# A two-layer hybrid decoder on one core: the order of the trunk's phases rewritten, and short attention tiles joined

## The reference, cut to what matters

```python
for l in range(DEPTH):
    h = rms_norm(x, norm1_w[l])
    proj = h @ w_in[l]
    z, xbc, dt_raw, sb_qkv, nsa_q, nsa_kv, nsa_gate = jnp.split(proj, IN_SPLITS, axis=-1)
    y_ssd = ssd_mixer(z, xbc, dt_raw, ...)                     # conv, state space scan in chunks of 128, gated norm
    y_sb = rms_norm(stick_breaking_attention(sb_qkv), ...)     # 4 heads
    y_nsa = rms_norm(nsa_attention(nsa_q, nsa_kv, ...), ...)   # compressed + selected + window branch, 4 heads
    x = x + jnp.concatenate([y_ssd, y_sb, y_nsa], axis=-1) @ w_out[l]
    x = x + peer_ffn(rms_norm(x, norm2_w[l]), ...)
```

## Time and profile before

| what | value |
|---|---|
| median of 3 runs | 3233.42 us (3232.33 to 3233.64) |
| the profiled execution | 3229.1 us, its span 3227.3 us |
| busy share of the span | PE 79%, DVE 75%, POOL 66%, ACT 25% |
| moved by DMA | 1187.51 MB, mean 368 GB/s; gathers 1073.87 MB of it |
| TensorE's granted clock, mean | 0.911 of 2.4 GHz |

### The profile page before, as it was taken

The page is one execution under the profiler, slowest core; times in us unless marked ns, Lnnn a source line. Parts: engine busy times, 40 slices in busy tenths (PEclk is TensorE's granted clock), DMA queues, the critical chain, the costliest instruction groups (busy, mean ns, idle before and its releaser), DMA issues. The chain is left out here.

```text
span 3227.3 us, 30187 instructions
## 1 busy us (share of the span) xinstructions
PE 2555.5 (79%) x8860; PEld 1512.6 (47%) x8860; DVE 2429.2 (75%) x5632; ACT 799.3 (25%) x1853; POOL 2115.9 (66%) x2059
## 2 busy tenths in 40 slices
PE   8877677898897686888788687899898587656667
PEld 7666433665464332665455342566566342222222
DVE  2324997768878997768878998758877999666664
ACT  2521222234321122223421122233431122111111
POOL 0001677657777777757776777766777777777775
PEclk9859799999898899898899799999899899998889
DMA  5104899999999999999999999999999999999999
GB/s 191 55 21 160 345 409 409 412 406 372 383 379 411 366 402 410 411 411 394 397 392 410 390 404 409 410 412 388 386 376 411 393 385 409 409 409 410 409 409 354
DMA packets 311313, 1187.51 MB, mean 368 GB/s; under 512 B 34544, under 2 KB 34544, under 8 KB 298352
## 3 DMA queue, kind: packets, MB, share of 16 engines
q0 software_dynamic: 294912, 1073.87, 84.7%
q1 hardware_dynamic: 16240, 111.72, 8.7%
HBM read 1183.36 MB, written 2.10 MB: 367 GB/s over the span
## 5 line engine op out<-in xcount | busy, mean ns | idle before, releaser
L754 PE MATMUL acc<-v_rows,diag 128*128 128x512 f32 x2728 | 1431.5, 659 | 485.7 <-DMA v_rows<-expert_v,idx 391.1
L1416 DVE CUSTOM_DVE_ANT_0 u_rows<-u_rows,h 128x1024 f32<-128x1024 f32 x1024 | 1231.4, 1216 | 398.4 <-DMA u_rows<-expert_u,idx 396.4
L1477 POOL DMA_INDIRECT u_rows<-expert_u,idx x1024 | 1057.0, 1032 | 625.6 <-DVE idx L1381 269.0
L1490 POOL DMA_INDIRECT v_rows<-expert_v,idx x1024 | 1057.2, 1032 | 425.6 <-issue 261.1
L754 PEld LDWEIGHTS acc<-v_rows,diag 128*128 128x128 f32 x2728 | 523.3, 207 | 1202.2 <-issue 985.4
L1434 DVE SCALAR_TENSOR_TENSOR X<-v_rows,wgt,X 128x1024 f32<-128x1024 f32 x342 | 439.2, 1284 | 43.5 <-DMA v_rows<-expert_v,idx 37.9
L1032 ACT ACTIVATE diag<-consts,wgt 128x128 f32<-128x128 f32 x682 | 255.1, 395 | 746.9 <-PE acc L754 567.9
L465 PE MATMUL bank<-HT,w_ring 128*128 128x256 f32 x1792 | 412.6, 386 | 2.2 <-DVE HT L1040 2.2
L465 PEld LDWEIGHTS bank<-HT,w_ring 128*128 128x128 f32 x1792 | 350.0, 196 | 93.3 <-issue 46.1
L474 PE MATMUL bank<-w_ring,HT 128*128 128x256 f32 (+1 forms) x1280 | 278.7, 375 | 2.6 <-ACT arena L765 2.6
L765 ACT ACTIVATE arena<-bank 128x256 f32<-128x256 f32 (+4 forms) x304 | 112.7, 382 | 664.5 <-PE bank L465 253.8
(11 more groups left out here) (185 smaller groups left out, 1990.6 us busy)
## 6 DMA issues: line engine op xcount, KB each, us to landing
w_ring<-weights SPq DMA_DIRECT2D x100, 1024.0 KB, 8.0
u_rows<-expert_u,idx POOLq DMA_INDIRECT x1024, 11.0
v_rows<-expert_v,idx POOLq DMA_INDIRECT x1024, 11.2
X<-in_x SPq DMA_DIRECT2D x2, 1024.0 KB, 6.6
out<-X SPq DMA_DIRECT2D x4, 512.0 KB, 6.6
n2w_wide<-parameters SPq DMA_DIRECT2D x2, 512.0 KB, 8.4
params<-parameters SPq DMA_DIRECT2D x2, 412.0 KB, 7.6
consts<-constants SPq DMA_DIRECT2D x1, 749.5 KB, 6.4
```

The lines of the kernel that those rows point to most:

```text
L754: last = T.matmul(acc[:, at_h], diag[:, i % DIAG_RING], v_rows[:, t % V_RING, at_h], start=(at_t == 0), stop=(t == max(q for q in range(t ...
L1416: made(V.tensor_tensor_reduce(out=rows_u, in0=rows_u, in1=h2[:], scale=1.0, scalar=0.0, op0=ALU.mult, op1=ALU.add, accum_out=dots[:, b % 2 ...
L1477: pool.indirect_dma_start(out=u_rows[:, s % U_RING, :], out_offset=None, in_=u_dram, in_offset=bass.IndirectOffsetOnAxis(ap=idx[:, n % 2, ...
L1490: pool.indirect_dma_start(out=v_rows[:, t % V_RING, :], out_offset=None, in_=v_dram, in_offset=bass.IndirectOffsetOnAxis(ap=idx[:, t // PE ...
```

## The change

It keeps the computation and rewrites the order, with what the order needs:

- `UNITS`: the projections come as keys and queries (`na`), stick-breaking q and k, the values, then the state space's features and the gate z; the weight slots are renumbered, and the compressed tokens' weights become slot 7 instead of 12.
- The evacuation of unit j becomes a phase of its own, `e{j}`, which may stand elsewhere than at `u{j+1}`.
- `phases(n)` has one list for step 0 (FIRST_UNITS, then FIRST_ATT with the attention tiles between its strings) and one for steps 1 to 3 (BESIDE_UNITS by pair, then BEFORE_ATT, then attention). Stick-breaking, keys and compressed tokens stand between the projections in all steps. In step 0 the state space's hops stand between the attention tiles; in steps 1 to 3 they stand ahead of them.
- `att_tiles`: in pair 0 tiles are joined, 4 heads of a 128-wide block or 2 heads of a 256-wide one, so 16 tiles become 6 (11 phases in place of 21); in pair 1 they stay 16. A tile's scores are now the mask first (one matmul over all its heads), then per head one matmul for the earlier columns and one for the block's own.
- Stick-breaking in pair 0: `sl` handles two heads at once (two Abs, two Exp, two Ln: one pair of table switches for two heads), and `wT` has two buffers.
- `y5`: the two Ln run together, then the two Exp; the norm of the sparse attention (`rstd("4")`) runs once for both blocks.
- Scratch tiles move to other memory, the compressed keys' sum takes the fourth bank, and some waits change with them (`cz` no longer waits for the state space's end; `de00` and `y5` wait for the compressed tokens).

The core of the diff:

```diff
-UNITS = ([("f", m) for m in range(8)] + [("z", 0, 0), ...] + [("f", m) for m in range(8, 12)]
-         + [("sv", 0), ("sv", 1), ("kv", 0), ("kv", 1)] + [("na", 0, 0), ...])
+UNITS = ([("na", 0, 0), ("na", 1, 0), ("na", 0, 1), ("na", 1, 1)] + [("f", m) for m in range(8, 12)]
+         + [("sv", 0), ("sv", 1), ("kv", 0), ("kv", 1)] + [("f", m) for m in range(8)]
+         + [("z", 0, 0), ("z", 1, 0), ("z", 0, 1), ("z", 1, 1)])
+FIRST_UNITS = (
+    "u0 u1 u2 u3 u4 np0 u5 np1 u6 np2 u7 np3 u8 np4 u9 sz0 sz1 nt0 u10 sl0 sl1 ne0 nt1 u11 sp0 sp1 ne1 u12 sr0 cz dt0 u13 sr1 se0 "
+    "cm0 cm1 cm2 cm3 se1 u14 so0 cr dt1 sw0 u15 so1 ct sz2 sz3 sw1 cv0 dt2 u16 sl2 sl3 k0 cv1 dt3 u17 sp2 sp3 k1 dt4 cv2 u18 sr2 k2 "
+    "dt5 cv3 u19 sr3 se2 kt cv4 se3 u20 so2 ke cv5 sw2 u21 so3 cs cv6 cs0 cs1 sw3 u22 cx0 cv7 cs2 cs3 cs4 u23 cs5 cs6 cs7 ca")
+BESIDE_UNITS = [
...
+    "u0 u1 u2 u3 u4 np0 u5 np1 u6 np2 u7 np3 u8 np4 u9 nt0 ne0 e9 u10 nt1 ne1 e10 cz sz0 u11 sl0 e11 dt0 sp0 u12 sr0 dt1 e12 se0 so0 "
+    "sz1 sw0 u13 sl1 dt2 e13 sp1 dt3 u14 dt4 sr1 e14 se1 dt5 cm0 cm1 cm2 cm3 cr so1 ct k0 sw1 sz2 u15 sl2 k1 cv0 e15 sp2 u16 sr2 cv1 k2 e16 "
...
+    "cv7 u22 e22 u23 e23 cs0 cs1 cs2 cs3 cs4 cs5 cs6 cs7"]
+BEFORE_ATT = ("xt0 dl00 xe0 de00 xt1 dl01 xe1 de01 xp0 xp1 cb0 dm0 yp0 ya0 dl10 ys0 st0 de10 su0 dl11 cb1 de11 dm1 yp1 ya1 st1 ys1 su1 "
+              "y2 y3 y5")
+FIRST_ATT = ["xt0 dl00", "xe0 de00 cx1 xt1 dl01", "xe1 de01 xp0 cp cb0", "xp1 dm0 ce yp0", "ya0 ys0 oc dl10", "og de10 dl11 st0",
+              "de11 su0 cb1", "dm1", "yp1", "ya1 ys1 st1", "su1 y2 y3", "y5"]
...
+        tiles = {1: [[0, 2, 4, 6], [1, 3, 5, 7]], 2: [[0, 2], [1, 3], [4, 6], [5, 7]]}.get(2 * p + b + 1, [[i] for i in range(8)])
...
-                        T.matmul(out[:, 0:width], nqT[base:base + 64, h // 2, blk[b]], nkT[base:base + 64, br, 0:width], start=True, stop=False)
-                        full(T.matmul(out[:, here[b]], ident, const("causal_neg"), start=False, stop=True), f"{n}.s{k}")
+                        T.matmul(out[:, :, here[b]], ident, const("causal_neg").unsqueeze(1).to_broadcast([P, len(heads), P]),
+                                 start=True, stop=False)
+                        for at_h, i in enumerate(heads):
+                            for cut in ([slice(0, width - P)] if width > P else []) + [here[b]]:
+                                last = T.matmul(out[:, at_h, cut], nqT[base:base + 64, i % NSA_H // 2, blk[b]],
+                                                nkT[base:base + 64, i // NSA_H, cut], start=False, stop=(...))
...
             def stick_l():
-                for h in range(SB_H):
-                    yield f"sl{h}"
+                at_once = 2 - p
+                for first in range(0, SB_H, at_once):
+                    yield f"sl{first + at_once - 1}"
```

More of the change, by code:

```diff
@@ L157, in phases @@
-def phases():
-    head = [("n1a", 0, .3), ("n1b", 0, 0), ("n1c", 0, .3), ("n1t0", 1.8, 0), ("n1t1", 1.8, 0), ("n1e0", 0, 1.3), ("n1e1", 0, 1.3)]
[L160 to L176, removed]
@@ new lines, in of_heads @@
+def of_heads(b, heads):
+    step = heads[1] - heads[0] if len(heads) > 1 else 1
+    return slice(8 * b + heads[0], 8 * b + heads[-1] + 1, step)
+ATT = [att_tiles(p) for p in range(PAIRS)]
+LAST_OF = [[max(k for k, tile in enumerate(ATT[p]) if tile[0] == b) for b in range(2)] for p in range(PAIRS)]
+FIRST_UNITS = (
[3 rows of a table added]
+BESIDE_UNITS = [
[8 rows of a table added]
+BEFORE_ATT = ("xt0 dl00 xe0 de00 xt1 dl01 xe1 de01 xp0 xp1 cb0 dm0 yp0 ya0 dl10 ys0 st0 de10 su0 dl11 cb1 de11 dm1 yp1 ya1 st1 ys1 su1 "
+              "y2 y3 y5")
@@ L186, in phases @@
     tail += [("g2", 0, .5)]
[L187 to L195, removed]
-def slots():
[L201 to L205, removed]
+    return head + costed(units) + att + tail
+PHASES = [phases(n) for n in range(STEPS)]
+ORDER = [{name: i for i, (name, *_) in enumerate(of_step)} for of_step in PHASES]
+assert all(len(a) == len(b) for a, b in zip(ORDER, PHASES))
+BEGINS = [0, *(int(n) for n in np.cumsum([len(of_step) for of_step in PHASES]))]
+def slots():
+    out = []
+    for n in range(STEPS):
+        first = ORDER[n]["r8"]
+        work = np.array([max(cost) + .5 for _, *cost in PHASES[n][:first]] + [cost[1] + .5 for _, *cost in PHASES[n][first:]])
+        spread = lambda part, lo, hi: lo + (np.cumsum(part) - part) / part.sum() * (hi - lo)
+        if n:
+            of_step = spread(work[:first], TRUNK_AT - PER_STEP, FIRST_AT - PER_STEP), spread(work[first:], FIRST_AT - PER_STEP, ROUTED_AT)
+        else:
+            of_step = np.full(first, -1), spread(work[first:], 1, ROUTED_AT)
+        out.append(n * PER_STEP + np.concatenate(of_step))
     return np.concatenate(out)
@@ L341, in take @@
                 n = free_in.index(min(free_in))
[L342 removed]
+                step = int(name.split(".")[0])
+                free_in[n] = BEGINS[step] + ORDER[step][done]
             if taken[n]:
@@ L527, in ssd, with states @@
                         full(last, f"{n}.l{b}{g_}")
+            def states():
+                for b in range(2):
                     yield f"cb{b}"
@@ L546, in ssd, with carried @@
                     full(last, f"{n}.yd{b}")
+            def carried():
+                for b in range(2):
+                    yield f"st{b}"
                     if 2 * p + b < BLOCKS - 1:
-                        out = take(pe, f"{n}.st{b}", f"ys{b}")
+                        out = take(pe, f"{n}.st{b}", f"su{b}")
                         wait_freed(pe, f"{n}.bt{b}")
@@ L637, in compressed @@
                                             start=(j == 0), stop=(j == CMP_LEN - 1))
-                            if j == CMP_LEN - 1:
-                                full(last, f"{n}.{name}")
+                            if j == CMP_LEN - 1 and name == "ck":
+                                made(last, "cmp_k")
+                            elif j == CMP_LEN - 1:
+                                full(last, f"{n}.cv")
                 yield "ct"
@@ new lines, in attention @@
+                        T.matmul(out[:, :, here[b]], ident, const("causal_neg").unsqueeze(1).to_broadcast([P, len(heads), P]),
[3 more added lines that the diff above has]
+                                last = T.matmul(out[:, at_h, cut], nqT[base:base + 64, i % NSA_H // 2, blk[b]],
+                                                nkT[base:base + 64, i // NSA_H, cut], start=False, stop=(at_h == len(heads) - 1 and cut == here[b]))
@@ L689, in attention @@
+                        full(last, f"{n}.s{k}")
+                    if 0 <= k - 3 < len(tiles):
                         j = k - 3
+                        b, heads = tiles[j]
                         out = take(pe, f"{n}.p{j}", f"t{j + 4}")
                         wait_freed(pe, f"{n}.s{j}")
-                        for kb in range(2 * p + j // (2 * NSA_H) + 1):
+                        for kb in range(len(heads) * (2 * p + b + 1)):
                             last = T.transpose(out[:, blk[kb]], probs[j % 2][:, blk[kb]], ident)
@@ L736, in out_ @@
                         full(last, f"{n}.sc{m}")
-            return [head(), ssd(), stick_z(), stick_r(), stick_o(), keys(), compressed(), attention(), out_()]
+            return [head(), ssd(), states_in(), decays(), states(), carried(), stick_z(), stick_r(), stick_o(), keys(), compressed(), attention(), out_()]
         def tensor_program(pe):
@@ L1195, in compressed @@
                 yield "cr"
+                dve.wait_ge(sig("cmp_k"), nth(n, "cmp_k", 1))
                 for i, name in enumerate(("ck", "cv")):
-                    bank = wait_full(dve, f"{n}.{name}")
+                    bank = banks[BANKS - 1] if name == "ck" else wait_full(dve, f"{n}.cv")
                     freed(V.tensor_copy(rep[0:64, i * P:(i + 1) * P].rearrange("p (a c) -> p a c", a=4),
```

213 lines of the change are left out of this document (133 added, 80 removed), and 5 rows, old and new, of the table BESIDE_UNITS.

## The result

| | median of runs | first gather of step 0's experts | from there to the end | span |
|---|---|---|---|---|
| before | 3232.88 us (4 runs) | 305.75 | 2921.6 | 3227.3 |
| after | 3192.56 us (4 runs) | 282.94 | 2907.2 | 3190.1 |
| after, run a second time with the last experiments | 3190.82 us (4 runs) | 278.30 | 2907.1 | 3185.4 |

The ratio of the times after to before is 0.9871, with an interval from 0.9856 to 0.9886: 40 us faster (predicted: 39). "First gather" is the time in the profiled execution at which DVE writes the first block of `h2`, the input of the experts (`h` in the rows; the gather itself is issued within about a microsecond of it); the last three columns are of that execution. They show where the time came from: 22.8 us of the span lie ahead of the first gather, 14.4 behind it.

A forecast was written before the change was run, and what follows sets the result against it. Step 0's trunk standing alone, then some 2900 us of gathers, bound the kernel. Step 0's -17 and steps 1 to 3's -22 gave -39 against the profiled 3229.1: 3190, or 3194 as median; range 3158 to 3228.

The forecast's parts named there:

- Step 0, last projection: Step 0, projections with hops between them: the last one ends at 139 us, expected within 133 to 142.
- Step 0, the joined stretch: Step 0, state space hops between joined attention tiles: 63 us, the middle of 51 at full and 76 at half clock.
- rival (b): Step 0's attention stretch: the clock drops and stays down, -3 - 22, total 3208 us; chance 0.12.
- The tail: Step 0, from the last attention tile to the output projection: 13 us, where it was 6.4 before.
- The term: Step 0's output projection starts at 215 us instead of 231.7: -17 us, bounds -32 and -3.
- rival (a): Step 0's attention stretch: the clock stays up, -32 - 22, total 3179 us; chance 0.20.
- the hops' part: Steps 1 to 3, 31 or 41 slots ahead of attention gain weight loads: 31 us, about two thirds taken, -22 us.
- the poor stretch is shorter, not poorer: Trunks beside gathers: GB/s stays at 410 some 90 us longer; the low-rate stretch shortens without a lower rate.
- the prediction's reason: Steps 1 to 3, where few weights load: gather issue limits, and DMA has room that weights could use.
- Rival (c): Trunks beside gathers give nothing, because DVE and PE waiting for each other limits them: -17, 3216 us; chance 0.12.
- Rival (d): Steps 1 to 3: the state space chain ahead of attention holds up gather buffers; slower, 3252 us; chance 0.07.
- (e): PE's order is new, but in-order bank waits grow until projections cover nothing: 3233 us; chance 0.04.

The follow-up runs named there:

- experiment 8: Changed kernel with attention of steps 1 to 3 over more slots, unused matmuls in step 0, first two heads' scores behind the twelfth projection: 3176.33 us, ratio 0.9832.
- Experiment 2: Changed kernel with step 0's state space hops ahead of attention instead of between its tiles: 3188.61 us, ratio 0.988.
- Experiment 7: Changed kernel with unused matmuls in step 0: 3186.97 us; with single tiles and three or one unused matmuls per attention step: 3217.55 and 3204.43 us.
- experiment 5: Changed kernel with the first eight weight loads of each of steps 1 to 3 cut to an eighth: 3144.16 us, ratio 0.9731.
- experiment 1: Changed kernel with the projections of steps 1 to 3 early and most hops behind them: 3265.39 us, 1.0114 times the kernel before.
- experiment 6: Changed kernel with attention of steps 1 to 3 spread over more slots: 3184.82 us, ratio 0.9858.
- experiments 3 and 4: Changed kernel with single attention tiles in steps 0 and 2: 3206.35 us; changed kernel with step 0's projections in one block, hops behind them: 3206.93 us.

## Why the prediction was right, and where it was not

- **Step 0, last projection: right.** 139 predicted with bounds of 133 to 142, 135.0 measured. The wait ahead of `u10` was 4.06 us (6 taken), at `cum` 2.15 (2.5 taken), and `u10` itself ran at half clock: 4.28 us for what took 2.18 in experiment 8, 2 of the 3 us charged. All waits of PE together were 7.2 us (10 taken), so most of the 4 us are waits.
- **Step 0, the joined stretch: right in length.** 195.8 - 135.0 = 60.8 us for the 63 taken, and the waits stood where it put them (the third tile's scores, `oc` and `dl`, the transposes of the fifth). The clock was 0.57 to 0.97 behind the projections, a mixture, though not always within the 0.6 to 0.9 forecast (rival (b) came for one window only). The 63 is the middle of 51 and 76, and the 71 us of work in the 76 are worked out from no row, so that the length came out is luck in part. Above 0.9 up to the last projection was missed in one window (0.86, at the wait ahead of `u10`). The tail was 13.9 us for 13. The term came to -21.9 at the output projection for the -17 predicted, mostly by the 4 us by which the projections ended earlier.
- **What the prediction did not see in step 0:** it treated the state space hops between the tiles as part of the gain. Experiment 2 shows no worth in that; joined tiles and stick-breaking between projections are worth 23 us together and 7 and 2 alone.
- **Full clock as rival (a):** it did not come, but its price was about right. With the clock at 1.00 from 100 to 225 us the output projection began at 201.8, -30 for the bound of -32. The first gather moved to 277.56, -28 against the kernel before, and by 5.4 and 0.7 us against the changed kernel's two profiles; the unused matmuls take some of PE's time themselves. The Trainium skill, "TensorE: Matmul & The Clock Gate", section "The HAM clock gate", says that activity releases the slow state. Experiment 7 agrees: with matmuls in PE's waits the clock stayed at 1.00 in windows that showed 0.57 and 0.91 without them.
- **Steps 1 to 3: the hops' part right in size, attention's part left out.** 14.4 us were measured for the 22. The step that failed is "the poor stretch is shorter, not poorer": the prediction put attention's stretch at no change, and it lost 30 us against 23 before. The hops' part, "31 x 0.33 + 41 x 0.25 + 31 x 0.35 = 31 us" with two thirds of it taken for -22, came to 22. That is luck in part: the two thirds are worked out from no row, and the 41 slots are 39 by its own slots (134 to 173).
- **The reason for the hops' part is not settled.** The change moves the weights and sets the hops further apart, both at once. For the prediction's reason, that weights fill room which gathers leave: POOL waited for no PE where experiment 5 cut the weights, and the rate fell to 386. And the gathers by themselves moved no faster beside the hops than before. Their bytes (the second number, MB) in 698 to 822 us before and in 543 to 800 us after make 361 and 356 GB/s; what was added is weights. In the kernel before, POOL hardly waited in the hops from 1500 to 1600 us (its largest wait for PE, the first line), and the rate was 389 all the same.

```profile
POOL v_rows L1490 <- PE acc L754: 1.2, 4, 0.3
...
q0 software_dynamic: 12292, 44.75, 94.8%
```

```profile
q0 software_dynamic: 25150, 91.59, 89.3%
```

- For the other reason, the spacing of the hops: experiment 1 set them close together and the rate fell to 245, with POOL waiting 24.1 us in 75; experiment 6 set attention's apart and its rate rose to 401. A run that cuts the loads behind the eighth, those that the change moved, would help to tell the two apart; there is none.
- **Rival (c)** did not hold as it stands, since the trunks gave 14.4 us. The waiting that it names (DVE and PE for each other) is real where pieces stand close, in experiment 1 and in attention. **Rival (d)**, the chain in front of attention, did not come: the stretch ahead of attention, up to 799 us, is at 410 GB/s. (e) fell with the trace.

The total came out within 2 us because 6 us too little up to the first gather (22.8 for 17) and 8 us too much behind it (14.4 for 22) offset each other. That is luck. In the second profile of the changed kernel it is 27.5 and 14.5.

## What to carry to other kernels

Where in-order engines hand small pieces to each other beside a stream of gathers, the spacing of the pieces can decide whether the stream stalls (experiments 1 and 6): put independent dense work between them, or leave more slots between them, and then look at the stretch behind, which can give back what was gained. Two edits that need each other are not to be priced one by one; take each back alone, as in experiments 3 and 4, before saying which is worth what. When a model gives the right total, test its terms: here the 14.4 us behind the first gather are 22 gained in one stretch and 8 lost in another that the model had left out. And before reading a run, look on its page for what its edit did: experiment 5 cut 8 loads of a step where 13 were meant.

## What was not expected of the hardware

The busy share of the DMA engines hardly tells whether they could move more: in attention's stretch it was 0.96 at 359 GB/s, ahead of it 1.02 at 410. Two executions of the same changed kernel were granted different clocks in the same stretch (0.57 and 0.73 from 150 to 175 us, 0.81 and 0.90 from 200 to 225), and their first gathers stood 4.6 us apart (282.94 and 278.30). So a difference of about 5 us at the first gather between two single profiles, such as experiment 7's 5.4, can't be told from that.
